# Latent attention of a two-block transformer kernel: full-precision products replaced by three single-pass products of high and low parts

## The reference

```
h = rms_norm(x, ln_mix[l])
parts of h @ w_in[l]: grouped-query q (8 x 64), k, v (2 x 64 each), latent q (256), latent kv (128) and a rotary key (32)
grouped-query branch: 8 heads, softmax attention over 512 tokens, heads of 64
latent branch:
  q  = rms_norm(latent q, mla_q_norm)  @ w_q_b    -> 8 heads x 96 (64 plain, 32 rotary)
  kv = rms_norm(latent kv, mla_kv_norm) @ w_kv_b  -> 8 heads x (64 key, 64 value)
  the last 32 of every query head and the one shared rotary key are rotated by the axial rope tables
  key head h = [64 of kv head h | shared rotary key]; softmax(q k^T / sqrt(96)) v, 8 heads
x = x + rms_norms of both branches, concatenated, @ w_o[l]
```

## Time and profile before

| | |
|---|---|
| median of 3 runs | 3003.81 us |
| lowest, highest | 3001.68, 3007.8 us |
| profiled execution: its own time and its span | 3003.8 us |
| PE busy in the span | 2816.4 us (94%) |
| DVE, ACT, POOL busy | 1422.1 (47%), 1129.1 (38%), 238.4 us (8%) |
| attention loop of layer 0, grouped-query part / latent part | about 79.5 to 153.8 us / 153.8 to 237.7 us |
| the same of layer 1 | about 738.5 to 812.8 us / 812.8 to 896.7 us |

### The profile page before, as it was taken

The page is one execution under the profiler, slowest core; times in us unless marked ns, Lnnn a source line. Parts: engine busy times, 40 slices in busy tenths (PEclk is TensorE's granted clock), DMA queues, the critical chain, the costliest instruction groups (busy, mean ns, idle before and its releaser), DMA issues.

```text
span 3003.8 us, 40104 instructions
## 1 busy us (share of the span) xinstructions
PE 2816.4 (94%) x16212; PEld 2094.2 (70%) x16212; DVE 1422.1 (47%) x2150; ACT 1129.1 (38%) x1920; POOL 238.4 (8%) x229
## 2 busy tenths in 40 slices
PE   7999979989999979999999789999999999799998
PEld 5657854536658745447877578888888787578886
DVE  6665532237666333244555763333334654753444
ACT  4664431124665321135233652222222542643332
POOL 0011020000011110001011010000001111000001
PEclk9999989999999989999999899999999999999999
DMA  4011249981002259993435122223320234222220
GB/s 157 29 43 59 86 173 415 415 366 64 29 29 100 100 237 418 414 395 127 144 115 153 40 76 113 112 114 128 124 84 16 88 122 130 81 84 99 98 99 28
DMA packets 67909, 428.28 MB, mean 143 GB/s; under 512 B 7968, under 2 KB 8352, under 8 KB 20368
## 3 DMA queue, kind: packets, MB, share of 16 engines
q1 hardware_dynamic: 62144, 407.96, 35.6%
q0 software_dynamic: 4432, 15.67, 1.6%
q10 hardware_dynamic: 1152, 2.10, 0.2%
HBM read 416.78 MB, written 8.91 MB: 142 GB/s over the span
## 4 chain that ended last, share of the span: by engine, by line
PE 82%; DVE 7%; DMA 4%; ACT 4%; issue 2%; POOL 2%; SPq 0%; DVEq 0%; ACTq 0%; POOLq 0%
PE banks L854 78%; PE banks L855 4%; DMA weight<-in_w_up 3%; ACT arena L1685 3%; DVE arena L2390 3%; POOL arena L3200 2%; DVE arena L3046 1%; DVE arena L2679 0%; DVE weight_part L2494 0%; DMA block_tokens_high<-df_stage 0%; DVE arena L2677 0%; DMA weight<-in_ada_w 0%; ACT weight_part L1685 0%; DVE x L2390 0%; POOL block_tokens_low L3214 0%
## 5 line engine op out<-in xcount | busy, mean ns | idle before, releaser
L1685 ACT ACTIVATE arena<-banks 128x512 f32<-128x512 f32 (+2 forms) x513 | 281.2, 550 | 885.0 <-PE banks L854 779.4
L854 PE MATMUL banks<-weight,arena 128*64 128x512 f32 (+4 forms) x2136 | 429.1, 573 | 21.3 <-DMA weight<-in_w_up 9.2
L854 PE MATMUL banks<-hidden,weight_part 128*128 128x512 f32 (+1 forms) x2304 | 446.8, 355 | 0.0
L854 PEld LDWEIGHTS banks<-hidden,weight_part 128*128 128x128 f32 x2304 | 381.2, 189 | 70.4 <-issue 3.8
L854 PE MATMUL banks<-tokens_high,weight_part 128*128 128x512 f32 (+1 forms) x1536 | 409.0, 357 | 10.0 <-ACT tokens_high L1685 10.0
L2494 DVE TENSOR_TENSOR weight_part<-weight,weight_part 128x2048 fp32r<-128x2048 f32 x124 | 285.8, 2308 | 194.8 <-ACT weight_part L1685 194.7
L1685 ACT ACTIVATE weight_part<-weight 128x2048 fp32r<-128x2048 f32 x124 | 236.4, 1908 | 349.7 <-PE banks L854 336.4
L854 PEld LDWEIGHTS banks<-weight,arena 128*64 128x64 f32 (+2 forms) x2136 | 150.9, 135 | 255.4 <-issue 233.8
L854 PEld LDWEIGHTS banks<-tokens_high,weight_part 128*128 128x128 f32 x1536 | 273.9, 190 | 62.5 <-DVE arena L2390 16.0
L3200 POOL TENSOR_TENSOR arena<-arena 128x512 f32<-128x512 f32 (+1 forms) x89 | 116.0, 1303 | 1974.3 <-ACT arena L1685 1707.4
L854 PE MATMUL banks<-tokens_low,weight_part 128*128 128x512 f32 (+1 forms) x768 | 264.7, 354 | 0.0
(11 more groups left out here) (216 smaller groups left out, 3879.6 us busy)
## 6 DMA issues: line engine op xcount, KB each, us to landing
weight<-in_w_gate SPq DMA_DIRECT2D x64, 1024.0 KB, 13.6
weight<-in_w_up SPq DMA_DIRECT2D x64, 1024.0 KB, 8.1
weight<-in_w_down SPq DMA_DIRECT2D x64, 1024.0 KB, 11.2
weight<-in_w_ff SPq DMA_DIRECT2D x64, 1024.0 KB, 4.8
weight<-in_ada_w SPq DMA_DIRECT2D x48, 1024.0 KB, 6.3
weight<-in_w_in SPq DMA_DIRECT2D x28, 1024.0 KB, 5.2
weight<-in_w_o SPq DMA_DIRECT2D x8, 1024.0 KB, 4.8
weight<-in_w_mem_kv SPq DMA_DIRECT2D x8, 1024.0 KB, 4.9
```

Source lines behind the costliest of these rows:

```text
L854: mm = lambda o, a, b, first=True, last=True: eng.matmul(o, a, b, start=first, stop=last, skip_group_check=True)
L1685: act = lambda o, i, f=ACT.Copy, **k: eng.activation(o, i, f, **k)
```

## The change

All operands of the latent branch are split into high and low parts, and every product becomes three single-pass products:

- `w_kv_b` and `w_q_b` join the split weights. `w_kv_b`'s columns are reordered on the host: all keys, then all values. `split_high`/`split_low` of `w_kv_b` stand where those of the first `w_o` chunk stood; those of `w_q_b` and of three `w_o` chunks follow in slots 6, 10, 27 and 30 (before: two `w_o` chunks at 6 and 10).
- The normalized latents are split: `CKH`, `CKL`, `CQH`, `CQL` (slots 3 to 6).
- `vm`, `qm`, `km` and the latent scores use `tile3`. One `km` now makes the keys of two heads (128 columns). Odd heads keep their rotary rows below their plain rows, with 32 rows of zeros, so an odd head's score product has 128 rows.
- Keys are kept as four high and four low tiles, `KMH` and `KML`, used by heads h and h+4. Their rotary rows are written once, in slots 5 and 6. The plain rows are rounded by ACT (`kmh`), and DVE subtracts (`keys_low`), reading the product's bank; the bank is freed by DVE's second subtraction.
- Queries: after `mla_rope`, ACT rounds (`mla_high`, two slots after the preparation) and DVE subtracts (`mla_low`, three slots after).
- `VM_AT` is 6; preparations: head 0 in slot 9, 1 in 11, 2 in 13, 3 in 15, 4 and 5 in 20, 6 and 7 in 24.
- On POOL the load of `mem` is issued after head 4 and no longer after head 2.

```diff
-        VM_AT = 4
-        PREP_AT = [NG - 4, NG - 2] + [NG + 4 * j + 2 * h for j in range(3) for h in range(2)]
+        VM_AT = 6
+        PREP_AT = {NG - 7: (0,), NG - 5: (1,), NG - 3: (2,), NG - 1: (3,), NG + 4: (4, 5), NG + 8: (6, 7)}
+        MIX_SPLITS = {6: ("w_q_b",), 10: ("w_o", 0), NG + 11: ("w_o", 1), NG + 14: ("w_o", 2)}
...
 PE:             def mla_prep(h):
-                    tile(("qm", l, h), [wq[:, k, P * h:P * h + P] for k in range(2)], [S["CQ"][:, k, :] for k in range(2)],
-                    tile(("km", l, h), [wkv[:, P * h:P * h + NOPE]], [S["CKV"]], rows=NOPE,
+                    tile3(("qm", l, h), [(qh[:, k, at], ql[:, k, at]) for k in range(2)], [(S["CQH"][:, k, :], S["CQL"][:, k, :]) for k in range(2)],
+                    if h % 2 == 0:
+                        at = slice(NOPE * h, NOPE * h + P)
+                        tile3(("km", l, h // 2), [(kh[:, at], kl[:, at])], [(S["CKH"], S["CKL"])],
 PE:             def mla_score(pu):
-                        tile(("S", u), [S["QM"].get((l, h))[0:QK, q * P:q * P + P]], [S["KM"].get((l, h))[0:QK, :]],
+                        r = slice(0, QK if h % 2 == 0 else P)
+                        query = S["QMH"][h][r, at], S["QML"][r, h % 4, at]
+                        keys = S["KMH"][r, h % 4, :], S["KML"][r, h % 4, :]
+                        tile3(("S", u), [query], [keys], free=(S["QM"].free((l, h)), ("keys_dead", l, h)) if q == TB - 1 else ())
...
 ACT:            def mla_prep(h):
                     copy(q, ("qm", l, h), PB.get(("qm", l, h)), ("qr", l, h), scale=QK ** -0.5)
-                    copy(m[0:NOPE, :], ("km", l, h), PB.get(("km", l, h))[0:NOPE, :])
-                    act(m[64:96, :], S["KR"][64:96, :]).then_inc(*done(("kmr", l, h)))
+                    if h % 2 == 0:
+                        for z in (h, h + 1):
+                            act(S["KMH"][r, z % 4, :], PB.get(("km", l, h // 2))[r, :]).then_inc(*done(("kmh", l, z)))
+                def mla_high(h):
+                    act(S["QMH"][h], S["QM"].get((l, h))).then_inc(*done(("qmh", l, h)))
...
 DVE:
+                def keys_low(h):
+                    key = ("km", l, h // 2)
+                    for z in (h, h + 1):
+                        r = nope_rows(z)
+                        eng.wait_ge(*after(("kmh", l, z)))
+                        tt(S["KML"][r, z % 4, :], PB.get(key)[r, :], S["KMH"][r, z % 4, :], SUB).then_inc(*done(("kml", l, z), *((PB.free(key),) if z % 2 else ())))
+                def mla_low(h):
+                    eng.wait_ge(*after(("qmh", l, h)))
+                    tt(S["QML"][:, h % 4, :], S["QM"].get((l, h)), S["QMH"][h], SUB).then_inc(*done(("qml", l, h)))
...
+                    if i == 5:
+                        tt(S["CKL"], S["CKV"], S["CKH"], SUB).then_inc(*done(("ckvl", l)))
+                        for z in (1, 3):
+                            eng.memset(S["KML"][0:32, z, :].bitcast(F32), 0.0).then_inc(*done())
+                            eng.memset(S["KMH"][0:32, z, :].bitcast(F32), 0.0).then_inc(*done())
+                    if i == 6:
+                        for k in range(2):
+                            tt(S["CQL"][:, k, :], S["CQ"][:, k, :], S["CQH"][:, k, :], SUB).then_inc(*done(("cql", l, k)))
+                        for z in range(4):
+                            tt(S["KML"][rope_rows(z), z, :], K[R, :], S["KMH"][R, 0, :], SUB).then_inc(*done(("kmr", l, z)))
+                    for h in PREP_AT.get(i - 3, ()):
+                        mla_low(h)
+                    for h in PREP_AT.get(i - 1, ()):
+                        mla_rope(h)
+                        if h % 2 == 0:
+                            keys_low(h)
```

More of the change, by code:

```diff
@@ L1067, in mla_prep @@
                     if h == 0:
[L1068 to L1075 removed]
+                        wcur[:] = [weight_parts(("w_q_b", l)), wcur[1]]
@@ new lines, in mla_prep @@
+                    (qh, ql), (kh, kl) = wcur
+                    at = slice(P * h, P * h + P)
+                    tile3(("qm", l, h), [(qh[:, k, at], ql[:, k, at]) for k in range(2)], [(S["CQH"][:, k, :], S["CQL"][:, k, :]) for k in range(2)],
+                          free=(WF(("w_q_b", l)),) if h == HQ - 1 else (), needs=[("cql", l, k) for k in range(2)])
+                    if h % 2 == 0:
+                        at = slice(NOPE * h, NOPE * h + P)
+                        tile3(("km", l, h // 2), [(kh[:, at], kl[:, at])], [(S["CKH"], S["CKL"])],
+                              free=(WF(("w_kv_b", l)),) if h == HQ - 2 else (), needs=[("ckvl", l)])
@@ L1095, in mix_between @@
                         if c == 0:
[L1096 to L1101 removed]
+                            wcur.append(weight_parts(("w_kv_b", l)))
+                        kh, kl = wcur[1]
+                        at = slice(c * P, c * P + P)
+                        tile3(("vm", l, c), [(S["CKH"][:, at], S["CKL"][:, at])], [(kh[:, 512:1024], kl[:, 512:1024])], needs=[("ckvl", l)])
+                    for h in PREP_AT.get(i, ()):
+                        mla_prep(h)
                     if i == NG + 6:
```

116 lines of the change are left out of this document (74 added, 42 removed).

## The result

The changed kernel takes **3025.6 us** (median of 5 runs, 3024.7 to 3032.8), the kernel before 3006.2 in the same comparison: ratio **1.007**, 95% interval 1.0059 to 1.0082. I predicted 3002.0 with a range to 3012. It is slower by 19.4 us, where I gave "slower" a chance of 0.24.

What follows compares the result with a forecast made beforehand. PE's work was taken to bound the attention. Per layer 15.1 us saved less 14.2 us of new waits leaves 0.9, so 1.8 us off 3003.8: 3002.0 us, range 2985 to 3012.

Steps and rivals of the forecast that it cites:

- wait of slot 1: Before slot 1's scores: a half-as-wide chunk's split on DVE should remove PE's 0.66 us wait, 0.7 us a layer.
- burst, slots 4 to 8: Rotations, zeroings, subtractions and a split queued on DVE ahead of the maxima stall PE 3.8 us a layer.
- What bounds the kernel now: In both attention halves PE is busy almost without a gap; a change is worth PE time saved less PE waits made.
- What the new products cost: Per layer, three-pass products save PE 3.2 us in scores, 9.7 in preparations and 1.5 in `vm`.
- rival C: Products no cheaper: three products bound by weight loads, scores save nothing, 6.4 us lost, 3008 us; chance 0.08.
- The bank of the key product: DVE's later second subtraction frees it: PE waits 2.0, 2.6, 2.7, 3.1 us at slots 10, 14, 21, 25; 10.4 a layer.
- I cost it at nothing: Slot 20: POOL's cosine for head 5 behind three additions delays slot 21's maxima, but costs PE no time.
- the sum itself: Per layer 15.1 us saved less 14.2 given back in waits, 0.9 net; 1.8 us over two layers.
- Rival B: DVE bounds the attention: subtractions and zeroings queued ahead of maxima add 5.2 us a layer, 3012 us; chance 0.20.
- My test: Forecast wrong if the four bank waits are under 1 us or PE's attention idle grows much more than 28 us.
- my own rule: Faster: A plus a tenth of the forecast's cases; slower: B, a twentieth of those and half of C.
- PE's four slots beside the burst: Slots 4 to 7: 14.1 us on PE (2.9 + 3.9 + 3.6 + 3.6) against DVE's 18.9 us.

Runs made afterwards that it cites:

- e_keys_first: Changed kernel with VectorE subtracting the keys' low parts before rotating the queries instead of after; 3002.8 us, ratio 0.9995 to the kernel before.
- e_burst: Changed kernel with the shared key's low parts moved from slot 6 to 8 and 9, four zeroings from slot 5 to 13 and 15; 3024.2 us.
- e_pool: Changed kernel with GpSimd multiplying head 5's query rotation before, not after, adding the first outputs' squares in slot 20; 3029.5 us.

## Why the prediction was wrong

Per layer, from the piece of layer 0:

| term | predicted | measured |
|---|---|---|
| PE work saved (scores, preparations, `vm`) | 14.4 | 14.2 |
| wait of slot 1 | 0.7 gone | 0.66 still there |
| burst, slots 4 to 8 | 3.8 | 3.6 |
| key bank, slots 10 and 14 | 4.6 | 5.0 |
| key bank, slots 21 and 25 | 5.8 | 8.4 |
| lower clock behind the waits | not in the sum | 7.0 |
| **net** | **0.9 faster** | **10.1 slower** |

The 7.0 is the sum of the three falls as read under e_keys_first, 2.8, 1.6 and 2.6. The 14.2 hangs on it: 149.5 less what is left of 142.2 without 7.0. The last 0.4 of the idle time is a wait behind ACT at 243.66, with no term in the sum; the measured terms add up to 10.2, the 0.1 is rounding.

- **What bounds the kernel now**: right. PE was the time, and what it waits for counted in full.
- **What the new products cost**: right in sum, by two misses that cancel, so partly by luck. A late latent slot is 3.49 us, these two rows of after apart, for 3.81 before, not 3.6:

```profile
224.86 0.50 PE L880 MATMUL banks<-mla_key_high,mla_query_high 96*128 96x512 f32 x1
...
228.35 0.50 PE L880 MATMUL banks<-mla_key_high,gqa_low 96*128 96x512 f32 x1
```

  So the scores save 0.32 a slot, 5.1 us a layer and not 3.2, and rival C is out. The Trainium skill (FP8 and Floating Point Precision, TensorE Precision Notes), with three passes kept of four, would give an estimate of 0.44 a slot; the trace doesn't reach it. Preparations and `vm` save 9.1 together, by difference, for the 11.2 forecast. The sum gave the 0.2 for entering and leaving a run to the scores alone, but a preparation pays it too: the scores of slots 10, 11 and 12 start at 132.96, 137.48 and 140.43, so a plain slot is 2.95 us and one with a query product 4.52, 1.57 more where the sum has 1.36.
- **The wait of slot 1**: wrong. The split is shorter, 1.23 us, but ACT's high part, for which VectorE waits behind it, was next in line, and the same 0.66 us stand in every version.
- **The burst**: right in its mechanism and in sum, 3.6 for 3.8, but not in its place: I had 2.7 at slot 7, 1.1 at slot 8 and nothing at slot 6, and it was 1.28, 1.36 and 0.94 at slots 6, 7 and 8. That the sums are so near is partly luck.
- **The bank of the key product**: right in its mechanism, place and order, and for slots 10 and 14 in its size (2.2 and 2.8 for 2.0 and 2.6). Slots 21 and 25 were mis-sized, 3.75 for 2.7 and 4.69 for 3.1. The step that failed is "I cost it at nothing", said of GpSimd in slot 20: I asked only whom its late cosine holds up, and not what VectorE's own operations cost beside it. A rotation operation took 1.64 us there for 0.69, and in slot 24 the norm's multiplications 4.80 for 2.74, beside GpSimd's rotation. Less these, 0.95 and 2.06, the two waits would be 2.8 and 2.6, an estimate and near what the sum has. The earlier trace rows had the sign of it, a mean of 803 ns for operations that take 0.69 alone in the earlier trace rows.
- **The step that failed most** is the sum itself: it adds what PE waits for at the length of the wait. A wait of 2.76 us and more cost 1.6 to 2.8 on top, since the granted clock fell behind it. This is 7.0 of the 11.0 us between 0.9 faster and 10.1 slower, the slots 21 and 25 are 2.6 and slot 1 is 0.7; the other terms make the rest. Before had no wait over 0.70 us in this stretch and the clock at 1.00, so nothing there showed the price, but the page's mean clock of 0.977 said that it falls elsewhere, and I didn't go and look at what stood ahead of it.
- **Rival B** had the right sign and the wrong mechanism: I had VectorE's load bound the stretch, 3012. One exchange of two lines with the same load gave 22.8 us back. Load matters only once the banks are right, in slots 26 to 29.
- My test, that PE's idle time in the two attentions would grow by much more than 28 us, came out: 2 x 17.4 is 35. VectorE's busy time grew by 43 us, not by the 34 I had.
- My chances don't follow from my own rule: it gives 0.40 for "same" and 0.26 for "slower", not 0.42 and 0.24. And PE's four slots beside the burst add up to 14.0 us, not 14.1. Neither changes the forecast.

## What to carry to other kernels

When a consumer that frees a PSUM bank moves from one engine to another, write down what is queued ahead of it there; the freeing operation goes first in that queue, and work that nobody waits for goes behind it. Cost a TensorE wait of some 3 us or more at its length and 1.6 to 2.8 us besides, which is what the clock cost here, and break down one long wait before several short ones. Spread preparatory VectorE work over slots with room, away from GpSimd operations when both operands lie in SBUF, and recount each slot's VectorE work against PE's slot after every move.

## What the runs showed of the hardware

- In both layers of all fourteen traces the granted clock fell to 0.50 behind every TensorE wait of 2.76 us or more in the attention (35 waits, 2.76 to 4.70), in the old kernel's products too, and behind none of 1.77 us or less. Between them length alone doesn't settle it. It stayed 1.00 behind 2.13 and 2.38; the wait of 2.20 us before slot 10 was followed by 0.50 in two of eight cases, both in layer 1 (e_burst, e_pool); and the wait of 2.0 us that stands behind the attention, 17 us after one of 1.26, in nine of 28. What does settle it was not tried. The case of e_pool, PE and then the stretch:

```profile
804.91 0.79 PE L880 MATMUL banks<-gqa_high 64*128 64x512 f32 x2 [2.21 <-DVE mla_key_low L2635]
...
805.00:807.00 2.00, 2.00 (x9) 1.28 (x10) 0.37 (x1) 0.21 (x1) 0.00 (x0) 0.50 0.00 0
```

- A fall cost 1.6 to 2.8 us of PE time, not by the length of the wait: 2.8 behind 2.80 us, 1.6 behind 3.75, 2.6 behind 4.69. It went with how long the clock stayed at 0.50: 1.6 to 1.8 us where that was some 3.4 us, 2.5 to 2.8 where it was some 6.8, the end of the wait included.
- VectorE operations with both operands in SBUF took 1.47 to 1.66 us instead of 0.69 beside GpSimd's additions, and four multiplications 4.80 instead of 2.74; those that read a bank were not slower.
- VectorE's time went by the columns, not the rows: a two-operand operation of 512 columns took 0.68 to 0.70 us on 32, 64 and 128 rows. Zeroing 32 x 512 took 0.485, 0.55 from start to start, for the 0.4 of the sum.
